# Attention stage: max taken inside the score instruction, scores of two heads paired on TensorE, probabilities divided on GpSimd, loop written out

## The reference, cut to what matters

```
# B: 8 query heads, 2 key/value heads of width 64, 128-token blocks, a band of 384 keys
s = einsum(q, k_band) * 64**-0.5 ; s = where(mask, s, -inf)
m = maximum(max(s), sink)
p = exp(s - m); p = p / (sum(p) + exp(sink - m)); o_b = (p @ v_band) * silu(zb)
# C: 4 heads of width 128, 256 memory keys
p = softmax(qc @ km.T * 128**-0.5); o_c = (p @ vm) * silu(zc)
```

## Time and profile before

| what | us |
|---|---|
| median of 3 runs | 2540.59 |
| the profiled execution | 2542.03 |
| its span | 2540.4 |
| TensorE busy | 2221.4 (87%) |
| VectorE busy | 1150.4 (45%) |
| ScalarE busy | 661.5 (26%) |
| GpSimd busy | 396.2 (16%) |

### The profile page before, as it was taken

How to read it: one execution, slowest core, us unless ns; L and a number is a source line. 1 busy time by engine, 2 the same in 40 slices (tenths; PEclk the granted TensorE clock), 3 DMA queues, 4 the chain that set the end, 5 groups by cost and what they waited for, 6 DMA issues and landing times. The chain is left out here.

```text
span 2540.4 us, 29851 instructions
## 1 busy us (share of the span) xinstructions
PE 2221.4 (87%) x11392; PEld 1842.1 (73%) x11392; DVE 1150.4 (45%) x1842; ACT 661.5 (26%) x1000; POOL 396.2 (16%) x251
## 2 busy tenths in 40 slices
PE   6999999999999999998259998999766664699998
PEld 6788888888888888886158887888644342588887
DVE  7744444433432112211457765666536665322322
ACT  5411111111111111110344443443224344211111
POOL 3200000000000000000175554555000000000000
PEclk9999999999999999999589999999958887799999
DMA  6422212122222222210212212220041112443432
GB/s 232 143 100 74 73 62 89 50 74 74 74 74 74 74 74 74 74 66 25 88 67 75 75 62 73 75 76 17 19 159 50 50 50 100 165 166 133 162 136 83
DMA packets 74056, 219.92 MB, mean 87 GB/s; under 512 B 7488, under 2 KB 25024, under 8 KB 69744
## 3 DMA queue, kind: packets, MB, share of 16 engines
q1 hardware_dynamic: 63136, 179.35, 20.9%
q0 software_dynamic: 10832, 39.39, 4.1%
HBM read 174.02 MB, written 44.70 MB: 86 GB/s over the span
## 5 line engine op out<-in xcount | busy, mean ns | idle before, releaser
L73 PE MATMUL pr_acc<-x_hi,pr_w_lo 128*128 128x512 f32 (+1 forms) x1760 | 675.9, 384 | 25.9 <-DVE pr_w_lo L386 23.4
L74 PE MATMUL pr_acc<-x_lo,pr_w_hi 128*128 128x512 f32 (+1 forms) x1760 | 674.4, 383 | 0.0
L75 PE MATMUL pr_acc<-x_hi,pr_w_hi 128*128 128x512 f32 (+1 forms) x1760 | 674.2, 383 | 0.0
L73 PEld LDWEIGHTS pr_acc<-x_hi,pr_w_lo 128*128 128x128 f32 x1760 | 334.2, 190 | 91.5 <-issue 27.1
L74 PEld LDWEIGHTS pr_acc<-x_lo,pr_w_hi 128*128 128x128 f32 x1760 | 334.4, 190 | 63.7 <-issue 0.2
L75 PEld LDWEIGHTS pr_acc<-x_hi,pr_w_hi 128*128 128x128 f32 x1760 | 334.4, 190 | 63.5
L314 ACT ACTIVATE pr_w_hi<-pr_w_raw 128x1024 fp32r<-128x1024 f32 x118 | 124.8, 1059 | 758.3 <-PE pr_acc L75 740.1
L464 DVE TENSOR_TENSOR pr_padded<-pr_acc,pr_rstd 128x512 f32<-128x512 f32 x80 | 55.2, 692 | 501.5 <-PE pr_acc L75 501.4
L73 PE MATMUL ou_acc<-ou_w_hi,ou_m_lo 128*128 128x512 f32 x512 | 200.0, 391 | 46.9 <-ACT ou_w_hi L1689 46.9
L74 PE MATMUL ou_acc<-ou_w_lo,ou_m_hi 128*128 128x512 f32 x512 | 199.9, 390 | 0.0
L75 PE MATMUL ou_acc<-ou_w_hi,ou_m_hi 128*128 128x512 f32 x512 | 199.7, 390 | 0.0
(11 more groups left out here) (218 smaller groups left out, 2745.4 us busy)
## 6 DMA issues: line engine op xcount, KB each, us to landing
pr_w_raw<-in_w_in SPq DMA_DIRECT2D x118, 512.0 KB, 4.8
ou_w_raw<-in_w_out SPq DMA_DIRECT2D x32, 1024.0 KB, 4.8
proj_scratch<-pr_res POOLq DMA_DIRECT2D x51, 512.0 KB, 4.6
dl_qk<-proj_scratch SPq DMA_DIRECT2D x8, 1024.0 KB, 5.0
dl_grow<-gate_rows SPq DMA_DIRECT2D x8, 1024.0 KB, 7.0
dl_brow<-gate_rows SPq DMA_DIRECT2D x8, 1024.0 KB, 9.9
ou_w_raw<-mixed_scratch SPq DMA_DIRECT2D x16, 512.0 KB, 4.8
ou_x_in<-in_x SPq DMA_DIRECT2D x8, 1024.0 KB, 7.1
```

Source lines behind the costliest of these rows:

```text
L73: pe.matmul(out, w_lo, x_hi, start=first, stop=False)
L74: pe.matmul(out, w_hi, x_lo, start=False, stop=False)
L75: return pe.matmul(out, w_hi, x_hi, start=False, stop=last)
```

## The change

The loop over blocks is written out for all eight, so indices are constants. In M(u) of B the pair of L1443 instructions and the max L1446 become two `tensor_tensor_reduce`, one a head: (score + mask) times the reciprocal norm, and its running max from -3e38 into `mx`. `k_pad` holds both key heads in one plane, and the scores of head g use partitions 64g to 64g+63 of the queries and keys alone. N(u) moves from VectorE to GpSimd. `v_win` and its copy go; the value products read `v_rows`. The stores of the results move from GpSimd to SyncE, behind the load of the next block and each behind its wait.

```diff
-        k_pad = n.sb("k_pad", [P, 2, SEQ + 2 * P])
+        k_pad = n.sb("k_pad", [P, SEQ + 2 * P])
-        v_win = n.sb("v_win", [P, 2, 3, P])
...
-        def blocks(eng, slot):
-            slot(0, 0, True, 0)
-            slot(1, 1, True, 1)
-            with eng.Fori(1, BLK // 2 - 1) as i:
-                slot(i * 2, 0, True, 1)
-                slot(i * 2 + 1, 1, True, 1)
-            slot(BLK - 2, 0, True, 1)
-            slot(BLK - 1, 1, False, 2)
+        LOWEST = -3e38
+        def blocks(slot):
+            for h in range(BLK):
+                slot(h, h % 2, h < BLK - 1, 0 if h == 0 else 2 if h == BLK - 1 else 1)
...
             load(0, 0)
-            blocks(sp, lambda h, parity, more, w: load(h + 1, 1 - parity) if more else None)
+            def slot(h, parity, more, w):
+                if more:
+                    load(h + 1, 1 - parity)
+                sp.wait_ge(b_res, h * 2 + 1)
+                sp.dma_start(mixed[...], out_b[:]).then_inc(st_b, 16)
+                sp.wait_ge(b_res, h * 2 + 2)
+                sp.dma_start(mixed[...], out_c[:]).then_inc(st_c, 16)
...
# GpSimd
             def slot(h, parity, more, w):
-                if after(h, 2):
-                    pool.wait_ge(b_o, h * 2 - 2)
-                pool.tensor_copy(v_win[:, parity], v_rows[:, bass.ds(h, 3)]).then_inc(b_win, 1)
-                ... (the two stores)
+                for u in range(U):
+                    odd = (parity + u) % 2
+                    if u < LAST:
+                        pool.wait_ge(b_d, h * 9 + (2 * u + 2))
+                        for i in range(2):
+                            part = prob[:, odd, i * W:i * W + W]
+                            pool.tensor_scalar(part, part, rsum[:, odd, i:i + 1], None, ALU.mult).then_inc(b_p, 1)
+                    else:
+                        pool.wait_ge(b_d, h * 9 + 9)
+                        for i in range(4):
+                            part = prob[:, odd, i * MEM_LEN:(i + 1) * MEM_LEN]
+                            pool.tensor_scalar(part, part, rsum[:, odd, i:i + 1], None, ALU.mult).then_inc(b_p, 1)
...
# VectorE, maxima
-                        dve.scalar_tensor_tensor(sm[:, odd, i], ps[:, odd, i, 0:W], rq[:, bass.ds(h, 1), 2 * u + i],
-                                                 window[:, which], ALU.mult, ALU.add).then_inc(b_a, 1)
+                        dve.tensor_tensor_reduce(sm[:, odd, i], ps[:, odd, i, 0:W], window[:, which],
+                                                 rq[:, h, 2 * u + i:2 * u + i + 1], LOWEST, ALU.add, ALU.max,
+                                                 mx[:, odd, i:i + 1]).then_inc(b_a, 1)
                     dve.wait_ge(b_a, h * 8 + (2 * u + 2))
-                    dve.tensor_reduce(mx[:, odd, 0:2], sm[:, odd], AX_X, ALU.max).then_inc(b_m, 1)
-                    dve.wait_ge(b_m, h * 6 + (u + 1))
...
# VectorE, probabilities: the multiplications L1470-L1472 and L1477-L1479 are gone, with the wait on b_d ahead of them
...
# TensorE, scores and values
-                        last = pe.matmul(ps[:, odd, g, 0:W], q_rope[:, parity, u], k_pad[:, g, bass.ds(h * P, W)],
+                        rows = slice(64 * g, 64 * g + 64)
+                        last = pe.matmul(ps[:, odd, g, 0:W], q_rope[rows, parity, u], k_pad[rows, bass.ds(h * P, W)],
                                          start=True, stop=True)
-                pe.wait_ge(b_win, h + 1)
-                        last = pe.matmul(po[64 * g:64 * g + 64, :], v_win[:, parity, kc, 64 * g:64 * g + 64],
+                        last = pe.matmul(po[64 * g:64 * g + 64, :], v_rows[:, h + kc, 64 * g:64 * g + 64],
```

More of the change, by code:

```diff
@@ L1296, in _ @@
             load(0, 0)
-            blocks(sp, lambda h, parity, more, w: load(h + 1, 1 - parity) if more else None)
+            def slot(h, parity, more, w):
+                if more:
+                    load(h + 1, 1 - parity)
+                sp.wait_ge(b_res, h * 2 + 1)
+                sp.dma_start(mixed[A_HEADS:A_HEADS + 4, :, bass.ds(h * P, P)].rearrange("a p n -> p a n"),
+                             out_b[:]).then_inc(st_b, 16)
+                sp.wait_ge(b_res, h * 2 + 2)
+                sp.dma_start(mixed[A_HEADS + 4:A_HEADS + 8, :, bass.ds(h * P, P)].rearrange("a p n -> p a n"),
+                             out_c[:]).then_inc(st_c, 16)
+            blocks(slot)
+            sp.wait_ge(st_b, 16 * BLK)
+            sp.wait_ge(st_c, 16 * BLK)
         @block.gpsimd
@@ L1351, in exps @@
                     act.wait_ge(b_n, h * 9 + (2 * u + 2))
-                    if not (isinstance(h, int) and h == 0 and u < 2):
+                    if not (h == 0 and u < 2):
                         act.wait_ge(b_t, h * 10 + (2 * u - 2))
@@ L1389, in _ @@
             exps(0, 0, 0, 0)
-            blocks(act, slot)
+            blocks(slot)
         @block.vector
@@ L1412, in _ @@
                 rows = slice(64 * g, 64 * g + 64)
-                dve.tensor_tensor(k_pad[rows, g, P:P + SEQ], k_in[rows, :], k_tmp[rows, :], ALU.add).then_inc(k_out, 1)
+                dve.tensor_tensor(k_pad[rows, P:P + SEQ], k_in[rows, :], k_tmp[rows, :], ALU.add).then_inc(k_out, 1)
             dve.wait_ge(p_root, 2)
@@ L1468, in probabilities @@
                     dve.reciprocal(rsum[:, odd, 0:2], rsum[:, odd, 0:2]).then_inc(b_d, 1)
[L1469 to L1472, removed]
                 else:
@@ L1475, in probabilities @@
                     dve.reciprocal(rsum[:, odd], rsum[:, odd]).then_inc(b_d, 1)
-                    dve.wait_ge(b_d, h * 9 + 9)
-                    for i in range(4):
-                        part = prob[:, odd, i * MEM_LEN:(i + 1) * MEM_LEN]
-                        dve.tensor_scalar(part, part, rsum[:, odd, i:i + 1], None, ALU.mult).then_inc(b_p, 1)
             def results(h, parity, which):
@@ L1503, in NEXT_WINDOW @@
             def NEXT_WINDOW(h):
-                return 2 if isinstance(h, int) and h == BLK - 2 else 1
+                return 2 if h == BLK - 2 else 1
             queries(0, 0)
             maxima(0, 0, 0, 0)
-            blocks(dve, slot)
+            blocks(slot)
         @block.tensor
@@ L1540, in _ @@
             pe.wait_ge(k_vd, 2)
+            pe.wait_ge(p_zero, 3)
             pe.wait_ge(p_w, 3)
@@ L1576, in transposes @@
                         pe.wait_ge(b_p, h * 12 + 12)
-                    if not (isinstance(h, int) and h == 0 and u == 0):
+                    if not (h == 0 and u == 0):
                         pe.wait_ge(b_td, h * 10 + (2 * u + i - 1))
@@ L1620, in _ @@
             scores(0, 1, 1, 0)
-            blocks(pe, slot)
+            blocks(slot)
 def output_stage(nc, c, mixed, w_out, x, out):
```

20 lines of the change are left out of this document (5 added, 15 removed).

## The result

The changed kernel takes 2573.68 us (median of 4 runs, 2570.91 to 2575.99); beside it the kernel before took 2539.47 (4 runs). The ratio is 1.0133, 95% interval 1.0117 to 1.0149: slower by 34 us, where 7 us faster was forecast and 2552 was the end of the range. The profiled execution took 2570.91 with a span of 2569.2 us; the traces of the two kernels are 28.8 us apart.

The account below looks back on a forecast made before the run. Prediction: a chain through engines binds the loop, mid-block by VectorE, start by a DMA, end by TensorE. Gains of 2.9 (block 0), 1.5 (blocks 1 to 6), 2.2 (block 7), 0.3 (last store) total 7 us: 2533.6 median, range 2519 to 2552.

Parts of the forecast that it names:

- I take 0.56 and 0.44, close to the copy, because both read one tensor.: GpSimd's price for one multiplication N of 384 and 256 elements, in us, taken from the 515 ns copy.
- The chain M(2) to X(4): Middle of a block, from masking M(2) through TensorE's order and N(4) to X(4): 13.4 us after, 14.04 before.
- The gain of 0.6: Us saved per block from M(2) to X(4): 0.75 from M(2), 0.7 from P(1) and S(4)'s delays, minus 0.6.
- rival (a): More comes out: cheaper instructions, no later load, X(1) and S(4) at 2.4 GHz; 20 us gained, 2521; chance 0.17.
- Rival (c), the clock: TensorE's idle gap ahead of X(4) passes 2.1, seven blocks pay 2.4 at the lower clock; 2551 to 2556; chance 0.21.
- 2.2 less was forecast: Block 7 has no queries, so M(1), P(0) and M(2) count until ScalarE's E and T hold: 2.2 us gained.
- VectorE's other savings lie beside this chain and bring nothing: VectorE's time falls 46 us in all, but savings off the way from M(2) to X(4) were given 0.
- The combined instruction, 1.3 a pair taken: VectorE's masking and max in one instruction: 1.3 us a pair, between bounds of 1.14 and 2.1.
- The start of a block: VectorE's 1.4 us saved there become wait for the queries, whose load comes 0.35 later; idle grows from 7.4 to 16.
- The pairs: Two heads' score products run at once, 0.65 us less per unit; only block 0's first is exposed, gaining 1.3.
- (d), the shared access: GpSimd and VectorE share SBUF access: 16% of N on the chain, 0.4 a block, 3 us; no chance of its own.

Follow-up runs that it names:

- The probe: The changed kernel with N on VectorE and eighteen GpSimd instructions of several forms added ahead of the attention loop: 2523.25 us, one run.
- the base: The changed kernel with one thing undone, the multiplications N back on VectorE: 2521.32 us, ratio 0.9913 to the kernel before.

## Why the prediction was wrong

- **The step that failed: "I take 0.56 and 0.44, close to the copy, because both read one tensor."** They take 1.25 and 0.93, above the dearest bound that I gave (1.02 and 0.68) as well. Number of inputs was the wrong likeness; the nearest rows by operation gave no price for this instruction at all. The Trainium skill (GPSIMD Engine Reference, section "Elementwise — side-by-side cycle accounting") gives 1.03 cycles an element for a body of one or two operations, by estimate 0.86 ns at the 1.2 GHz of that section. The probe's copies agree (504 and 402 ns for 384 and 256 elements, 0.80 ns an element); the multiplication by a scalar, at 2.50 ns, does not. The rule of the Trainium skill in that section, that elementwise work belongs to VectorE, is borne out.
- **The chain M(2) to X(4): 13.4 forecast, 16.7 measured.** Step by step in block 3: X(1) starts at 3.22 instead of 2.86; to the end of S(4) 5.54 instead of 4.1, because X(1)'s second half starts 1.22 after the first, behind the second multiplication, and S(4) takes 3.62 for 2.78; N(4) starts 0.3 late behind N(3) and takes 3.63 for 1.76. The 14.04 that the prediction takes for before is the mean of two blocks; over blocks 0 to 6 it is 14.3, so the chain grew by 2.4 a block. The gain of 0.6 is the difference of the two totals; the parts named for it (0.75 + 0.7 - 0.6) make 0.85, and those of rival (a) make 1.8 to 2.3 a block, not 2 to 2.5. The structure of the sum held: with VectorE's prices for N (X(1) at 2.34, N(4) with handover 1.2, and without the 0.2 added) it gives 11.9, and the base measures 12.1 on the mean of blocks 0 to 6. What I did not do is this very sum. It would have said that the move costs 1.5 a block even at my prices.
- **Rival (c), the clock, with a chance of 0.21, is what happened, on top of a price it was not given.** Its condition (0.65 or more for 256) was met. Values took 3.3 or more in six of eight blocks (4.49, 4.49, 2.80, 3.33, 4.89, 2.79, 3.31, 4.93). It was priced at 2551 to 2556 because it went with 0.8 a block for dearer multiplications; by block 3 they cost 2.8 (0.36, then about 0.6, then 1.87). Its reason does not hold as stated. It let the clock fall where the wait right ahead of X(4) passes 2.1. Block 2 has such a wait, and X(4) and values run at 2.4 GHz:
```profile
1995.33 1.09 PE L1585 MATMUL at_tp<-c_ident,at_prob 128*128 128x128 f32 x8 [2.21 <-POOL at_prob L1325]
1996.35 2.80 PE L1594 MATMUL at_po<-at_pt_b,at_v_rows 128*64 128x512 f32 x12
```
  So does X(4) in blocks 0, 1 and 5, behind 2.21 each. In blocks 3, 4 and 6 the wait is only 1.12, and there X(4) takes 1.97: the scores ahead of it had already run slower (1.65 for four matmuls instead of 0.92). The wait right ahead does not tell the clock in these rows.
- **The miss in numbers: 40 us between the medians (2573.7 against 2533.6), 36 between the profiled executions (2570.9 against 2535.0).** The rows place the 36. The chain, 3.3 in each of seven blocks, makes 23. Block 7, from the results of C of block 6 to X(4), takes 19.3 where it took 16.5 and 2.2 less was forecast, 5. Values take 31.0 for 23.9, 7, and X(4) 12.3 for 9.6, 3. That is 38, and behind the last result of C the kernel is 2.7 shorter than before. Of the 38 the clock has 13, by estimate: the 7, the 3, and 3 in S(4) (25.6 for the 8 x 2.78 of the forecast). The other 25 are price.
- **"VectorE's other savings lie beside this chain and bring nothing" was wrong.** The combined instruction gives 27 us, about 3 a block. Block 7, from which I took E(4) until the reciprocal (2.32), has no M(0) behind M(4); in the other blocks P(4) stood behind M(0), and its max counted too. So that saving entered my sum unseen, and I named it nothing.
- **The combined instruction, 1.3 a pair taken: 1.19** (2011.13 to 2012.32), at the lower bound.
- **The start of a block: right.** VectorE's idle before the queries grew from 7.4 to 18.3 (16 or more forecast). The queries came 0.2 later behind the results in block 2, but on the mean of six blocks no later (5.48, before 5.47; 0.35 taken).
- **The pairs: right in size** (block 0 gained 1.27, 1.3 forecast; 0.92 for four matmuls, 0.8 forecast), and worth nothing in the time.
- **(d), the shared access:** found where I did not put it, in a small VectorE instruction, at most 4.9 us.

## What to carry to other kernels

A work item that moves to a slower engine is priced twice: by its duration in the very form of instruction it will have there (GpSimd's multiplication by a scalar costs 2.5 times its copy, 3 times VectorE's), and by the idle time that it brings into TensorE's work, in which the granted clock fell here (0.88 to 0.75 over the loop) and made the next steps dearer too. Work the sum for the change without each of its parts before forecasting the whole: here one part was worth -27 us, one +52 to +56, and the others together some +5. An engine with 45% of the span busy still bound the loop's middle, and what freed it was fewer passes over the data, not another engine.

## What the runs showed of the hardware

- GpSimd multiplying 128 rows by a scalar: 1.25, 0.93 and 0.60 us for 384, 256 and 128 elements; by a constant 1.17 for 384. The two-input instruction with the scalar spread over the row is faster, 0.83 (0.84 and 0.61 for 384 and 256 in the loop); two whole tiles 1.00, a copy 0.50.
- One VectorE instruction that scales, masks and takes the row maximum: 0.61 for 384 elements and 0.08 for reading out the maximum, as much as masking alone; the second of a pair starts 0.53 after the first.
- More TensorE work that nobody needs made the kernel faster, in two kernels: by 22.6 us in the changed kernel (fillers; granted clock of the loop 0.75 to 0.89), and with early queries by 8.8 (fillers; 0.88 to 0.96) and 6.7 (zeros in the keys; 0.88 to 0.95).
- S(4), X(4) and values took 68.9 us in the changed kernel, 54.8 in the base and 46.2 in the changed kernel with fillers, for the same matmuls. X(4) ran at 2.4 GHz behind a wait of 2.21 and at 1.2 GHz behind one of 1.12.
